# The last step of a plain feed-forward by halves of the tokens, and another order of the next layer's first units

## The reference

```python
def swiglu(x, w_in, w_down):
    gate, up = jnp.split(x @ w_in, 2, axis=-1)
    return (jax.nn.silu(gate) * up) @ w_down

for i in range(DEPTH):                       # DEPTH = 4
    kind, j = i % N_MIXERS, i // N_MIXERS    # gdn, hgrn, gla, gdn
    ...
    x = layer_norm(DN_ALPHA * x + m, mix_ln_g[i], mix_ln_b[i])
    x = layer_norm(DN_ALPHA * x + swiglu(x, ffn_w_in[i], ffn_w_down[i]), ffn_ln_g[i], ffn_ln_b[i])
```

## Time and profile before

| | us |
|---|---|
| median of 3 runs | 2134.87 |
| lowest and highest | 2132.56, 2137.17 |
| the profiled execution | 2137.8 |
| its span, first to last instruction | 2136.1 |
| PE, DVE, ACT busy in it | 2077.8, 1488.5, 891.5 |

### The profile page before, as it was taken

The page is one execution under the profiler, slowest core; times in us unless marked ns, Lnnn a source line. Parts: engine busy times, 40 slices in busy tenths (PEclk is TensorE's granted clock), DMA queues, the critical chain, the costliest instruction groups (busy, mean ns, idle before and its releaser), DMA issues.

```text
span 2136.1 us, 35611 instructions
## 1 busy us (share of the span) xinstructions
PE 2077.8 (97%) x14377; PEld 1805.2 (85%) x14377; DVE 1488.5 (70%) x1941; ACT 891.5 (42%) x1174; POOL 177.8 (8%) x152
## 2 busy tenths in 40 slices
PE   7999999999999999999899999999989999999999
PEld 7988888798888798888798878887869998778998
DVE  5957754778854677744696685456688877588887
ACT  2254444334434423444323454445554334663332
POOL 5720000000000000000063300000100000100000
PEclk9999999999999999999999999999999999999999
DMA  7511655553555553555464046554325555414552
GB/s 227 178 61 61 205 189 191 170 190 99 180 196 182 173 178 119 197 192 182 139 180 155 3 149 216 186 186 154 103 78 171 186 183 170 138 50 158 194 180 99
DMA packets 267625, 333.81 MB, mean 156 GB/s; under 512 B 20562, under 2 KB 230613, under 8 KB 267493
## 3 DMA queue, kind: packets, MB, share of 16 engines
q1 hardware_dynamic: 267493, 331.93, 47.8%
HBM read 330.84 MB, written 1.05 MB: 155 GB/s over the span
## 4 chain that ended last, share of the span: by engine, by line
PE 86%; DVE 8%; ACT 3%; issue 2%; SPq 1%; DMA 0%; DVEq 0%; ACTq 0%
PE bank L586 45%; PE bank L554 29%; PE bank L1056 2%; DVE w_lo L2225 1%; ACT stat L1579 1%; PE bank L820 1%; PE bank L637 1%; DVE sq L2184 1%; PE bank L912 1%; PE bank L982 1%; PE bank L1137 1%; DVE pj L2184 1%; PE bank L926 1%; DVE xt L2184 1%; ACT w_hi L1624 1%
## 5 line engine op out<-in xcount | busy, mean ns | idle before, releaser
L2225 DVE TENSOR_TENSOR w_lo<-ring,w_hi 128x2048 fp32r<-128x2048 f32 (+2 forms) x289 | 615.2, 2131 | 375.3 <-ACT w_hi L1624 372.9
L1624 ACT ACTIVATE w_hi<-ring 128x2048 fp32r<-128x2048 f32 (+1 forms) x220 | 418.9, 1905 | 472.6 <-PE bank L586 287.3
L586 PE MATMUL bank<-w_lo,xh 128*128 128x512 f32 x992 | 267.7, 393 | 0.0
L554 PE MATMUL bank<-xh,w_hi 128*128 128x256 f32 x1752 | 239.9, 290 | 5.8 <-DVE w_hi L2223 5.0
L554 PE MATMUL bank<-xh,w_lo 128*128 128x256 f32 (+2 forms) x1832 | 242.4, 285 | 0.0
L586 PE MATMUL bank<-w_hi,xl 128*128 128x512 f32 x896 | 240.6, 390 | 1.0 <-DVE xl L2174 0.9
L586 PE MATMUL bank<-w_hi,xh 128*128 128x512 f32 x896 | 240.9, 391 | 0.6 <-ACT xh L1579 0.6
L554 PEld LDWEIGHTS bank<-xh,w_hi 128*128 128x128 f32 x1752 | 225.0, 195 | 15.8 <-issue 10.2
L554 PEld LDWEIGHTS bank<-xh,w_lo 128*128 128x128 f32 (+2 forms) x1832 | 229.1, 191 | 1.3
L554 PE MATMUL bank<-xl,w_hi 128*128 128x256 f32 x1752 | 230.1, 284 | 0.0
L554 PEld LDWEIGHTS bank<-xl,w_hi 128*128 128x128 f32 x1752 | 219.2, 192 | 0.4
(11 more groups left out here) (323 smaller groups left out, 2406.0 us busy)
## 6 DMA issues: line engine op xcount, KB each, us to landing
ring<-in_ffn_w_in_dram SPq DMA_DIRECT2D x264, 512.0 KB, 4.4
ring<-in_ffn_w_down_dram SPq DMA_DIRECT2D x88, 512.0 KB, 4.1
ring<-in_gdn_w_in_dram SPq DMA_DIRECT2D x64, 512.0 KB, 5.0
ring<-in_ffn_w_out_dram SPq DMA_DIRECT2D x44, 512.0 KB, 3.9
ring<-in_w_in_dram SPq DMA_DIRECT2D x40, 512.0 KB, 4.7
ring<-in_hgrn_w_in_dram SPq DMA_DIRECT2D x32, 512.0 KB, 4.5
ring<-in_gla_w_in_dram SPq DMA_DIRECT2D x24, 512.0 KB, 4.6
ring<-in_gdn_w_out_dram SPq DMA_DIRECT2D x16, 512.0 KB, 4.5
```

The costliest lines, as they stand in the source:

```text
L554: m = nc.tensor.matmul(cols, *((wk, xk) if tokens == ALL else (xk, wk)), start=(first and step == 0 and k == 0 and (j % 2 == 0)), stop=(la ...
L586: m = nc.tensor.matmul(bank[:, 0:width], xin[:, k0 + k, rows_of], w[:, k, c * width:(c + 1) * width], start=(first and step == 0 and k == ...
L1624: nc.scalar.activation(taken(high_part(u), u), taken(ring[:, u % RING, :], u), ACT.Copy).then_inc(*act_hi.tick())
L2225: v.tensor_tensor(w_lo[:, u % RING, 0:share], w[:, 0:share], high[:, 0:share], ALU.subtract).then_inc(*dve_lo.tick())
```

## The change

In the four plain feed-forwards, step 10 and the last two down products become one routine `last_step` on PE, ACT and DVE. PE runs the "gate" and "up" units for the first half of the tokens, then "gate" for the second, transposes the first half's hidden rows, runs "up" for the second, and so on; `hid_hi` and `hid_lo` are made for each half apart. Both last down products are then run for t = 0, and after that for t = 1. Before layers 1 and 2 (hgrn, gla) the transposes of the norm's part (0,0) are moved ahead of the last 6 matmuls of the feed-forward, into bank 7. In the list `order` the next layer's first unit changes places with the last down product, and the split of the next layer's second unit moves from before the norm into it. `last_downs` now serves only the second block, where nothing changes.

```diff
--- before.py
+++ after.py
@@ -438,7 +438,9 @@
             for n in range(3 * F_STEPS):
                 unit_plan(SLOT, "act", 8)
                 hi_slot.append((1 - turn, EXTRA)[n] if n < 2 else (n - turn) % HI)
-            order += range(first, first + n_in + 4)
+            if 0 < layer <= DEPTH:
+                order.insert(len(order) - 1, first)
+            order += range(first + (0 < layer <= DEPTH), first + n_in + 4)
             f0 = first + n_in + 4
             order += [f0 + 1, f0, *range(f0 + 2, f0 + 3 * F_STEPS)]
         slot_before, last_in, rank = [], {}, {"act": {}, "dve": {}, "low": {}, "pool": {}}
@@ -613,7 +615,7 @@
             def pair_after_norm(u, banks_, norm, keys, third):
 
 
-                half_after_norm(u, banks_[0], 0, norm,
+                half_after_norm(u, banks_[0], 0, norm, left_came=(third is not None),
                                 before_last=None if third is not None else lambda: rows_to_channels(norm, 1, 0))
                 if third is not None:
                     ahead(u + 2, third, norm)
@@ -755,8 +757,6 @@
 
                 nonlocal unit
 
-                early = layer >= DEPTH
-
                 def rows_of(n, t, c):
                     return token_products(unit + n, banks[2 * t + c], t, 0, 2, (hid_hi[:, 1 - n], hid_lo[:, 1 - n]), c=c,
                                           first=False, last=(n == 1))
@@ -767,16 +767,57 @@
                 if between:
                     between()
                 rows_of(0, 1, 0)
-                if early:
-                    rows_of(0, 1, 1).then_inc(*pe_unit.tick("down", layer, 9))
+                rows_of(0, 1, 1).then_inc(*pe_unit.tick("down", layer, 9))
                 pe.wait_ge(*ready[1])
                 for c in range(2):
                     rows_of(1, 0, c).then_inc(*pe_norm.tick("down", layer, 0, c))
-                if not early:
-                    rows_of(0, 1, 1).then_inc(*pe_unit.tick("down", layer, 9))
                 rows_of(1, 1, 0).then_inc(*pe_norm.tick("down", layer, 1, 0))
                 rows_of(1, 1, 1).then_inc(*pe_unit.tick("down", layer, "last"))
                 unit += 2
+
+            def last_step(layer, freed, ninth_low):
+
+
+                nonlocal unit
+                gate, down9, down10 = unit, unit + 2, unit + 3
+
+                def gate_rows(t, kh):
+                    return token_products(gate + kh, banks[4 + t], t, 4 * kh, 4, (xh, xl), first=(kh == 0), last=(kh == 1))
+
+                def hidden_rows(t):
+                    pe.wait_ge(*dve_ffn.at("hidden", layer, 10, t))
+                    for j in range(2):
+                        m = nc.tensor.transpose(banks[6][:, j * T + t * HALF:j * T + (t + 1) * HALF],
+                                                hidt[:, t, j * P:(j + 1) * P], ident[:, :])
+                    m.then_inc(*pe_ffn.tick("hidden T", layer, 10, t))
+
+                def down_rows(u, par_, t, c):
+                    return token_products(u, banks[2 * t + c], t, 0, 2, (hid_hi[:, par_], hid_lo[:, par_]), c=c,
+                                          first=False, last=(u == down10))
+
+                for f in freed:
+                    pe.wait_ge(*f)
+                gate_rows(0, 0)
+                gate_rows(0, 1).then_inc(*pe_ffn.tick("half", layer, 10))
+                gate_rows(1, 0).then_inc(*pe_unit.tick("gate", layer, 10))
+                pe.wait_ge(*ninth_low)
+                hidden_rows(0)
+                gate_rows(1, 1).then_inc(*pe_unit.tick("up", layer, 10))
+                for c in range(2):
+                    down_rows(down9, 1, 0, c)
+                hidden_rows(1)
+                pe.wait_ge(*dve_ffn.at("hidden lo", layer, 10, 0))
+                for c in range(2):
+                    down_rows(down10, 0, 0, c).then_inc(*pe_norm.tick("down", layer, 0, c))
+                for c in range(2):
+                    m = down_rows(down9, 1, 1, c)
+                m.then_inc(*pe_unit.tick("down", layer, 9))
+                pe.wait_ge(*dve_ffn.at("hidden lo", layer, 10, 1))
+                down_rows(down10, 0, 1, 0).then_inc(*pe_norm.tick("down", layer, 1, 0))
+                if CHAIN[layer + 1][0] in ("hgrn", "gla"):
+                    rows_to_channels(2 * layer + 1, 0, 0, 7)
+                down_rows(down10, 0, 1, 1).then_inc(*pe_unit.tick("down", layer, "last"))
+                unit += 4
 
             def ffn(layer, norm):
 
@@ -847,8 +888,7 @@
                 unit = u0 + RING * F_PAIRS
                 gate_up(9, None, used("b"))
                 step_down(0, 8, None, low("b"), between=hidden_to_channels(9))
-                gate_up(10, None, used(9))
-                last_downs(layer, (low(9), low(10)), between=hidden_to_channels(10))
+                last_step(layer, used(9), low(9))
 
             def conv_ffn(layer, norm):
 
@@ -1869,8 +1909,24 @@
                 if layer == 0:
                     act.wait_ge(*dve_setup.at("angles"))
                     run(act_setup, flat(trig), flat(trig), ACT.Sin, "trig")
-                step(0, 10)
+
+                def gated(t):
+                    act.wait_ge(*(pe_ffn.at("half", layer, 10) if t == 0 else pe_unit.at("up", layer, 10)))
+                    run(act_ffn, gactt[:, t, :], banks[4 + t][:, 0:T], ACT.Silu, "gated", layer, 10, t)
+
+                def hidden_high(t):
+                    act.wait_ge(*pe_ffn.at("hidden T", layer, 10, t))
+                    of = slice(t * HALF, (t + 1) * HALF)
+                    run(act_ffn, hid_hi[:, 0, :, of], banks[6][:, :].rearrange("p (j n) -> p j n", j=2)[:, :, of], ACT.Copy,
+                        "hidden hi", layer, 10, t)
+
+                gated(0)
                 cast()
+                hidden_high(0)
+                cast()
+                gated(1)
+                cast()
+                hidden_high(1)
 
             def conv_ffn(layer):
 
@@ -2446,11 +2502,14 @@
                 if key[0] == "out":
                     split(2)
                 to_rms, all_at_once = next_kind == "four", next_kind == "gdn"
+                later = key[0] == "down"
                 chunk(0, 0)
                 chunk(0, 1)
                 mean(0)
                 normed(0, 0)
                 normed(0, 1)
+                if later and not all_at_once and not to_rms:
+                    split()
                 chunk(1, 0)
                 if to_rms:
                     dve.wait_ge(*gains_loaded(n + 1))
@@ -2472,6 +2531,8 @@
                     low_rows(n, 0, 0)
                     low_rows(n, 0, 1)
                 last = n + 1 if to_rms else n
+                if later and (all_at_once or to_rms):
+                    split()
                 low_rows(last, 1, 0)
                 low_rows(last, 1, 1)
                 split()
@@ -2538,6 +2599,24 @@
                         split()
 
 
+                def last_step(layer):
+                    def gated(t):
+                        dve.wait_ge(*act_ffn.at("gated", layer, 10, t))
+                        tt(s, hidt[:, t, :], gactt[:, t, :], banks[4 + t][:, T:2 * T], ALU.mult, "hidden", layer, 10, t)
+
+                    def low(t):
+                        dve.wait_ge(*act_ffn.at("hidden hi", layer, 10, t))
+                        of = slice(t * HALF, (t + 1) * HALF)
+                        tt(s, hid_lo[:, 0, :, of], banks[6][:, :].rearrange("p (j n) -> p j n", j=2)[:, :, of], hid_hi[:, 0, :, of],
+                           ALU.subtract, "hidden lo", layer, 10, t)
+
+                    gated(0)
+                    split()
+                    low(0)
+                    gated(1)
+                    split()
+                    low(1)
+
                 step(0, 0, None, 0)
                 for k in (1, 2):
                     step(k % 2, k, None, 2 * k)
@@ -2553,9 +2632,10 @@
                 unit = u0 + RING * F_PAIRS
                 step(1, 9, None, 18)
                 split()
-                step(0, 10, None, 20)
-                if not conv_ffn:
-                    split()
+                if conv_ffn:
+                    step(0, 10, None, 20)
+                else:
+                    last_step(layer)
                 dve.wait_ge(*s.now())
                 for b in range(4, 8):
                     psum.release(s, "ffn", layer, b)
```

## The result

The changed kernel took 2140.57 us (median of 14 runs, 2137.6 to 2143.21) against 2135.69 (14 runs, 2132.56 to 2138.77) for the kernel before: ratio 1.002, 95% interval 1.0013 to 1.0027. A second, separate measurement gave 1.0016 (1.0007 to 1.0026). It is slower by 3 to 6 us, about the 0.2% that can be told from no change. The predicted range, 2132.5 to 2141.0, holds it. The predicted 2137.5 us is 3.1 us too low, and 0.8 us of that is the kernel before, which takes 2135.69 us by 14 runs where the prediction had 2134.87 by three. A ratio of 1.002 stands on the line that the prediction drew between no change (chance 0.72) and slower (0.20).

What follows compares the result with a forecast made beforehand. PE was taken to bound the kernel, busy for 2077.8 of 2136.1 us. Terms +5.1 (layers 1, 2), -1.9 (layer 3) and -0.6 (layer 4) gave +2.6 us on the 2134.87 median: 2137.5 us, range 2132.5 to 2141.0.

Steps and rivals of the forecast that it cites:

- The chain's lead: After each plain feed-forward's halved last step, the norm's chain on DVE starts 3.1 us earlier.
- the four small fixed parts: In the halved step, DVE and ACT pay one fixed part more each per two halves, 0.2 us, hidden.
- Bank 7: Layers 1 and 2: the first product waits for DVE's xl to free the bank, 1.05 us later per layer.
- Rival (c): Bank 7 does not hold PE, so layers 1 and 2 gain 1.35 us each: 2129.7 us, chance 0.08.
- The clock: Layers 1 and 2: the clock falls behind PE's 3.15 us gap, costing 1.5 us per layer, bounds 0 and 3.4.
- (a): The clock holds in one or both of layers 1 and 2: 2134.5 to 2136.0 us, chance 0.28.
- (b): Clock falls for double length or in layer 4 too, or layer 3's gain is lost: 2141.3 with the first, chance 0.17.
- The sum for both layers: Layers 1 and 2 together: later first product plus clock loss, 2 x (1.05 + 1.5) = +5.1 us.
- the two waits of the earlier trace: PE waits of 2.66 and 2.30 us: the second was read as agreeing with the skill's clock rule, the first not.
- Layer 3: Before the second GDN layer: 3.1 us lead less 1.2 for ACT's cast, a gain of 1.9 us, bounds 0 and 3.1.
- ACT's cast: Before layer 3: the third unit's cast now precedes the second reciprocal root and gives back 1.2 us.
- Layer 4: Before the four mixers: a gain of 0.6 us, the product behind T10 waiting for the split; bounds 2.0 gained, 1.2 lost.

Runs made afterwards that it cites:

- e1: The changed kernel, but in layers 1 and 2 bank 7 is claimed behind the second norm pair, not before the first product: 2134.14 us, ratio 0.9987.
- e4: The changed kernel with six needless small matmuls into bank 4 in PE's gap before the first product of layers 1 and 2: 2138.69 us, ratio 1.0014.
- e6: The changed kernel run again unchanged, for a second profiled execution: 2141.02 us, ratio 1.0016 to the kernel before.
- e7: The change in layers 2 and 3 alone, layers 0 and 1 as in the kernel before: 2135.79 us, ratio 0.9989.
- e2: The changed kernel with the norm's first transposes in layers 1 and 2 back behind the whole feed-forward, in bank 0: 2133.30 us, ratio 0.9985.
- e11: The kernel before, undivided last step, with the low part of the second unit of layers 1 to 4 given to GpSimd: 2134.06 us, ratio 0.9985.

## Why the prediction was right, and where a size was off

**The chain's lead.** 3.1 us predicted, 3.16 measured; d10 starts after 14.0 us where the sum had 14.2, no wait for `hid_lo` is left, and the four small fixed parts are hidden.

**Bank 7.** Right, and shown: +1.05 us per layer was predicted; the first product came 26.20 us into the step against 24.97, so +1.2. e1 takes it away by the claim alone. Rival (c), that the bank doesn't hold PE, is out. Its arithmetic was sound: it gave 1.35 us less per layer for a PE that isn't held, and e1, which builds that case, has 1.4 and 1.6 less. A part of the 0.2 us that the sum lacked is the wait itself: `xl` ends at 408.57 and PE starts at 408.93, 0.36 us later.

**The clock.** Predicted 1.5 per layer with bounds of 0 and 3.4. The first trace had 4.87 us from first product to second unit where it was 3.28, so 1.6; e4 gives back 1.6. And the bounds were real: e6 has 3.4 in one layer and 0 in the other. Rivals (a) and (b) were two faces of one uncertainty, which came out differently in two executions of the changed kernel. The sum for both layers, +5.1, stands against +5.4 and +5.0 in the traces and 5.8 by e7. The Trainium skill (TensorE: Matmul & The Clock Gate, "Why this matters for your kernels") warns of this gap, and three of the four 3.3 us gaps in the two traces agree with it; the fourth kept its clock. The table speaks of longer gaps than the two waits of the earlier trace rows, so neither of them agrees or disagrees with it, contrary to the prediction's reading. But behind the 2.14 us wait before layer 4, or still in it, the clock was at half in all seven traces that have it, and that goes beyond the table.

**Layer 3.** Predicted -1.9. T10 came 27.21 us into the step against 29.51 before, -2.3. With the clock's share, up to the second unit, it was -2.7 in the first trace, and -1.8 to -2.7 with a mean of -2.5 in the seven traces with this chain. The predicted gain was 0.6 us too small. Two of the seven lost 1.7 us of clock there and five 3.4, but the length alone does not decide. What also seems to count is how much of the low clock lies in PE's idle gap. Here are e2, where it begins 1.4 us ahead of T10 (-2.7), and e7, where it begins 0.7 us behind T10 (-1.8); T10 stands at 1055.83 and 1056.37:

```profile
1054.00:1056.00 2.00, 0.17 (x1) 0.59 1.01 331
```

```profile
1056.00:1058.00 2.00, 0.81 (x5) 0.78 0.27 83
```

ACT's cast costs DVE 0.90 us, where I had 1.2.

**Layer 4.** Predicted -0.6, measured -0.1 and +0.3. In this term one step failed: the wait for the split came as forecast (2.14 us for 2.4), and T10 was 3.8 us sooner in its step, so that the product behind it started 1.45 us sooner. But from there to the next unit's product it took 5.79 us where it had taken 4.40: the clock fell again right behind the wait. The prediction named that fall as a bound and did not take it. A second fall, behind T00's shorter wait, came too:

```profile
1454.00:1456.00 2.00, 2.00 (x7) 0.52 0.84 268
1456.00:1458.00 2.00, 2.00 (x8) 0.63 0.00 0
...
1464.00:1466.00 2.00, 1.69 (x4) 0.58 0.00 0
1466.00:1468.00 2.00, 2.00 (x7) 0.57 0.00 0
```

Each costs 1.7 us, together as much as the single long one of 3.4 in the kernel before.

**The 2 us between the forecast and the median.** By the traces the sum was right: +2.6 predicted, +2.4 and +3.2 in the four pieces of the two traces. Some of that is luck, since layer 3 gained 0.6 us more than its term and layer 4 about 0.6 less. The medians differ by 4.9. Both profiled executions of before lay above the medians of their runs, by 2.1 and 1.6 us (2137.8 and 2138.31 against 2135.69 and 2136.67), those of the changed kernel near theirs (2140.15 and 2141.64 against 2140.57 and 2141.02). Over the 75 runs of before in the experiments, those with a mean granted clock of 0.994 took 2134.4 us on average, those with 0.991 2138.8. So a run's time goes with its clock falls, and a profile is one draw. Where in the kernel the 2 us lie is not shown, since runs without a profile have no record by place. One guess is that layers 3 and 4 gain less in typical runs than the 2.5 us of the sum: e7's medians give 1.1 us, but their interval reaches from 0.4 to 4.3.

## What to carry to other kernels

When a transpose or product is moved ahead of work that it does not depend on, look up which buffer it lands in and who next claims that buffer: here one early claim turned a lead of 3.1 us into a loss of 1.2 us and a clock fall, and moving the claim alone made a gain of 1.4 to 1.6 us per layer of it. A lead on one engine is worth only as much as the queue of the next lets through; the 2.28 us split had cost 0.4 to 1.3 us per layer where it stood before (e11), and given to an idle engine at 5.24 us, with the claim late or early, it turned a change that lost 0.2% into one that gains 0.5%. Price a gap in TensorE as a range (here 0, 1.7 or 3.4 us), not as one number.
